# Decoder stage of a YOCO-style step: projection units spread over twenty steps, value pages asked for one loop sooner

## The reference, cut to what matters

```python
D_MODEL, SEQ, DEC_BATCH, PAST_LEN, PAGE_SIZE = 1024, 512, 8, 2048, 128
H_B, DH_B, DV_B = 8, 64, 128          # heads, size of each of the two key maps, size of a value

kv = modulate(x, sh, sc) @ w_kv        # shared keys and values of prompt and samples
q = (modulate(x, sh1, sc1) @ w_q_b).reshape(n, t, H_B, 2 * DH_B) * (DH_B ** -0.5)

def page_step(carry, xs):              # samples: 16 pages each, of 128 positions
    phys, j = xs
    kpos = j * PAGE_SIZE + jnp.arange(PAGE_SIZE)
    dist = (qpos[:, None] - kpos[None, :]).astype(jnp.float32)
    bias = -slopes[:, None, None] * dist
    return update(carry, cache_k[phys], cache_v[phys], bias), None
...
m1, l1, a1, m2, l2, a2 = update(carry, k_new, v_new, bias)
o = a1 / l1[..., None] - lam * (a2 / l2[..., None])
```

## Time and profile before

| what | value |
|---|---|
| median of 3 runs | 1935.73 us (1934.38 to 1936.28) |
| time of the profiled execution | 1931.71 us |
| its span | 1929.8 us |
| mean granted TensorE clock | 0.885 |
| PE busy | 1521.2 us (79%) |
| DVE busy | 733.9 us (38%) |
| ACT busy | 418.1 us (22%) |
| POOL busy | 349.3 us (18%) |
| DMA | 551.66 MB, mean 286 GB/s |

### The profile page before, as it was taken

How to read it: one execution, slowest core, us unless ns; L and a number is a source line. 1 busy time by engine, 2 the same in 40 slices (tenths; PEclk the granted TensorE clock), 3 DMA queues, 4 the chain that set the end, 5 groups by cost and what they waited for, 6 DMA issues and landing times. The chain is left out here.

```text
span 1929.8 us, 22099 instructions
## 1 busy us (share of the span) xinstructions
PE 1521.2 (79%) x7374; PEld 709.2 (37%) x7375; DVE 733.9 (38%) x1284; ACT 418.1 (22%) x908; POOL 349.3 (18%) x270
## 2 busy tenths in 40 slices
PE   5899986695689999646999887777596599989950
PEld 2333335142333333203466563444343233333320
DVE  1001127675300000075846577995275300000018
ACT  1001014221121222222120002334431021212222
POOL 0000000000100000033735566650000000000004
PEclk8999998597799999967999997888798699999985
DMA  8572604604599999699789999985503499999962
GB/s 314 225 275 111 263 36 152 233 23 185 224 425 422 392 382 427 275 370 344 276 306 402 408 383 412 351 316 182 186 17 129 188 417 384 418 420 400 430 242 89
DMA packets 123149, 551.66 MB, mean 286 GB/s; under 512 B 16469, under 2 KB 46022, under 8 KB 101419
## 3 DMA queue, kind: packets, MB, share of 16 engines
q1 hardware_dynamic: 94530, 492.46, 64.4%
q10 hardware_dynamic: 19584, 37.28, 5.1%
q0 software_dynamic: 8944, 20.76, 3.0%
HBM read 521.82 MB, written 40.03 MB: 291 GB/s over the span
## 5 line engine op out<-in xcount | busy, mean ns | idle before, releaser
L1576 PE MATMUL ps<-arena_w,arena_r 128*64 128x512 f32 x1600 | 361.7, 608 | 28.8 <-issue 23.9
L1576 PEld LDWEIGHTS ps<-arena_w,arena_r 128*64 128x64 f32 x1600 | 121.1, 140 | 262.6 <-issue 256.5
L1558 PE MATMUL ps<-arena_w,arena_r 128*64 128x512 f32 x800 | 181.5, 601 | 19.4 <-ACT arena_r L1606 19.4
L1653 DVE TENSOR_TENSOR arena_r<-arena_r,ps 128x512 f32<-128x512 f32 x38 | 26.1, 687 | 419.1 <-ACT arena_r L1623 419.1
L1959 POOL TENSOR_TENSOR arena_w<-arena_w,arena_r 128x1024 f32<-128x1024 f32 x48 | 115.5, 2409 | 104.0 <-DMA arena_w<-in_cache_k_dram 103.7
L1959 POOL TENSOR_TENSOR arena_r<-arena_r 128x1024 f32<-128x1024 f32 x48 | 115.9, 2418 | 54.7 <-DMA arena_r<-in_cache_k_dram 54.6
L2012 PE MATMUL ps<-arena_w,xt 128*128 128x256 f32 x512 | 123.4, 403 | 1.4 <-ACT xt L2185 1.4
L450 PE MATMUL ps<-arena_w,xt 128*128 128x512 f32 x256 | 113.8, 600 | 1.0 <-DVE arena_w L531 0.6
L1070 PE MATMUL ps<-arena_w,xt 128*128 128x512 f32 x256 | 111.4, 593 | 0.0
L2012 PEld LDWEIGHTS ps<-arena_w,xt 128*128 128x128 f32 x512 | 102.5, 203 | 17.9 <-ACT xt L2185 1.5
L1507 POOL COPY small<-idx 128x1 int32 (+1 forms) x38 | 7.0, 184 | 516.9 <-PE ps L1524 456.0
(11 more groups left out here) (384 smaller groups left out, 1969.5 us busy)
## 6 DMA issues: line engine op xcount, KB each, us to landing
arena_w<-in_w_exp_gate_dram SPq DMA_DIRECT2D x38, 2048.0 KB, 13.6
arena_w<-in_w_exp_up_dram SPq DMA_DIRECT2D x38, 2048.0 KB, 19.1
arena_w<-in_w_exp_down_dram SPq DMA_DIRECT2D x38, 2048.0 KB, 17.5
arena_m<-in_cache_v_dram SPq DMA_DIRECT2D x128, 512.0 KB, 7.0
arena_w<-in_cache_k_dram SPq DMA_DIRECT2D x64, 512.0 KB, 9.0
arena_r<-in_cache_k_dram SPq DMA_DIRECT2D x64, 512.0 KB, 8.4
arena_w<-in_w_ada_dram SPq DMA_DIRECT2D x12, 2048.0 KB, 17.6
arena_m<-in_w_ada_dram SPq DMA_DIRECT2D x12, 2048.0 KB, 9.2
```

What stands on the lines that cost most here:

```text
L1558: last = nc.tensor.matmul(psy[c][at:at + 64, :], ht[u][:, k, 64 * (1 - a):64 * (2 - a)], wd[u][:, k, c * 512:(c + 1) * 512], start=(k == 0 ...
L1576: last = nc.tensor.matmul(ps[at:at + 64, :], xgt[u][:, k, 64 * a:64 * (a + 1)], w[u][:, k, :], start=(k == 0), stop=(k == KT - 1), tile_po ...
L1653: V.tensor_tensor(hs[u], es[u], psu[:, :], ALU.mult).then_inc(h_ok, 1)
```

## The change

`projected` is another table: step g now holds unit g-1 for g up to 5 (before: one unit at step 1, two at each of steps 2 to 5), and the other 19 units are spread over steps 6 to 20, one each, but two at steps 9, 13, 17 and 20 (before: one each at steps 6 to 20). All 24 units are still done at step 20.

In SP's loop g value group g-5 is asked for rather than g-6, and the loops end one sooner. The wait for `own_parts` is split: ahead of loop 5 for ten of them, ahead of loop 6 for all twelve. The buffers, the waits of `load_key` and `load_value`, and the steps at which PE uses the values are as before.

```diff
     def projected(self, g):
 
-        n = 2 * g - 1 if g <= 5 else g + 4
-        return range(max(n - (1 if g <= 1 or g > 5 else 2), 0), min(n, 24))
+        count = lambda g: min(g, 5) + max(min(g, 20) - 5, 0) * 19 // 15
+        return range(count(g - 1), count(g)) if g >= 1 else ()
...
-            for g in range(2, NKQ + LAG):
-                if g == LAG:
-                    sp.wait_ge(sp_mm, NCH)
+            for g in range(2, NKQ + LAG - 1):
+                v = g - LAG + 1
+                if v in (0, 1):
+                    sp.wait_ge(sp_mm, NCH - 2 + 2 * v)
                 for j in range(GRP):
                     if g < NKQ:
                         load_key(GRP * g + j)
-                    if g >= LAG:
-                        load_value(GRP * (g - LAG) + j)
-                if g >= LAG and (g - LAG) % 4 == 2:
-                    b = (g - LAG) // 4
+                    if v >= 0:
+                        load_value(GRP * v + j)
+                if v >= 0 and v % 4 == 2:
+                    b = v // 4
                     if b == 0:
                         sp.wait_ge(nv_out, 32)
                     sp.dma_start(vn, m.newD[1][b:b + 1, :]).then_inc(vn_in, 16)
```

## The result

The changed kernel takes 2015.0 us (median of 3 runs, 2012.6 to 2016.83), against 1935.73 before: a ratio of 1.0413 (95% interval 1.0393 to 1.0434), 79.3 us slower. The profiled execution took 2012.6 us, its span is 2010.7, its mean granted clock 0.866 (before 0.885). The forecast was 1988, so the direction held and the loss was half again as large as its +52.8; the time lies 3 us inside the upper end of the range, 2018.

What follows compares the result with a forecast made beforehand. The prediction took full DMA engines to bound steps 9 to 20 and DVE the later steps. Its terms, 39.8 + 5 + 3 + 5 = +52.8 us on 1935.7, gave 1988 us, range 1950 to 2018.

Steps and rivals of the forecast that it cites:

- The start: Start of the stage: fewer units at steps 3 and 4 let SP resume at 961.4 instead of 973.9, gaining 12 us.
- E6: End of PE's values in step 6, the first values of the stage: forecast at 977.5.
- R: Time from end of values in step g-1 to PE's possible start of step g+1: 18.5 us, bounds 15.9 and 22.6.
- Step 9: Eight transpositions and two units, with ACT's copies behind the exponent: values end at 1041.5, before 1036.1.
- E8: End of PE's values in step 8: E6 + R + 9.4, forecast at 1005.4.
- The clock: PE units behind long waits run slower, about one more such unit per group: 3 x 1.5, +5 us (0 to 8).
- Behind step 20: Later multiplication at the end of step 21, +5 us (4 to 8), and later keys afterwards, +3 (0 to 8).
- E20: End of PE's values in step 20: 1206.8, before 1167.0, +39.8 us (bounds +29.4 and +56.2).
- Faster: Rival: DMA alone sets the pace and the hole at the start stays closed, 1917 to 1923 us; chance 0.09.
- No change: Rival: the gain at the start and the coupling cancel, R about 9, 1936 us; chance 0.02.
- mild: Rival: ACT isn't held at step 9 and groups take 53 us instead of 59, about +25, 1961 us; chance 0.13.
- Worse than the bounds: Rival: keys late at every attention step too, one us at each of 15 steps, +95, 2031 us; chance 0.04.

Runs made afterwards that it cites:

- e2: The kernel before with only the change's new SP queue (queue only), its old table of units kept: 1989.76 us, ratio 1.0293.
- e8: The changed kernel, but loop g asks for key pages 4g+1 to 4g+4 and then for its four value pages: 1956.31 us, ratio 1.0109.
- e3: The changed kernel, but each loop asks for its four key pages first, then its four value pages (keys first): 1989.31 us, ratio 1.0284.
- e4: The changed kernel with the first double step at 7 instead of 9, leaving one unit at step 9: 1990.41 us, ratio 1.0289.
- table only: The kernel before with only the change's new table of projection units, SP's queue as before: 1941.31 us, ratio 1.0038.

## Why the prediction was right, and where its size was off

**The chain.** It was named as it is: values of step g-1, keys of step g and the first of g+1 behind them in SP's queue, sums, `biggest`, PE's step g+1. e2 shows that the queue edit alone closes it, e8 that taking the keys out from behind the wait opens it, e3 that both the four keys and the fifth must come out. Most signs forecast came: value pages asked for in loop 5, ACT idle over 8 us ahead of step 9's `exponent` (12.46), groups of four steps longer than 50 us (61.1 and 69.0, forecast 59.2). PE's waits for `biggest` at steps 8, 12, 16 and 20 were forecast at some 9 us and were 11.76, 10.49, 19.42 and 11.68. The DMA share was 0.75, not 0.85. SP's waits came to 209.4 us, but the forecast "from 73 us to well over 120" started from the wrong number: both kinds of wait were 111.1 us to 1360 (117.3 to 1440), so before as well SP ran against PE more than the prediction says, and just over 120 would have been no sign.

**The start.** SP resumed at 969.41, not 961.4. The stage itself began 2.6 us later in this run. PE's step 3 is not in this path, since PE waited 5.42 us for `biggest` behind it. But `biggest`, which the prediction took over from before, ended 5.7 us later (957.67 instead of 951.96), 3.1 of them beyond the stage's own; and the unit of step 4 took 9.33 us instead of 7.0:

```profile
957.73 0.38 PE L2051 MATMUL ps<-ident,small 128*16 128x128 f32 x1 [5.42 <-DVE small L2361]
957.90 9.33 PE L2005 MATMUL ps<-xt,arena_w 128*128 128x512 f32 x16
```

E6 was 985.5 instead of 977.5: 5.4 us of the miss, after taking off the 2.6. The 3.1 us arise ahead of what the change touches. Eight small operations of DVE in step 1 (L2473), beside GpSimd's multiplications, took 12.87 us in this run and 12.88 in those of queue only and keys ahead, but 8.24 to 8.26 in before and in the six others. After and keys ahead have the latest step 6 of all kernels with the new table (89.7 and 91.0 in the table above). What decides between the two lengths is open.

**R, the term that was mis-sized.** The term that failed is "from the multiplication to the end of `common` 2.8", used for every return, and with it the 18.5 taken for R. Steps 8, 12, 16 and 20 wait for `biggest`, whose tail behind that multiplication is longer: a sum, a one-row copy (L2358), an addition and the maximum. Row by row for step 12 (the fifth key issued, its multiplication, the maximum, PE):

```profile
1074.01 0.36 SPq L1893 DMA_DIRECT2D arena_w<-in_cache_k_dram  x1
...
1080.82 1.22 DVE L2340 TENSOR_TENSOR arena_w<-arena_w,arena_r 128x1024 f32<-128x1024 f32 x1 [2.46 <-DMA arena_w<-in_cache_k_dram]
...
1084.32 0.61 DVE L2361 TENSOR_REDUCE small<-arena_r 128x16 f32<-128x272 f32 x1
...
1084.98 0.38 PE L2051 MATMUL ps<-ident,small 128*16 128x128 f32 x1 [10.49 <-DVE small L2361]
```

| before step | values end to fifth key issued | to its multiplication | to the end of `biggest` | R |
|---|---|---|---|---|
| 8 | 8.4 | 6.3 | 6.1 | 20.9 |
| 12 | 8.7 | 6.8 | 4.1 | 19.7 |
| 16 | 11.0 | 11.4 | 6.1 | 28.6 |
| 20 | 9.0 | 6.2 | 6.1 | 21.3 |
| mean | 9.3 | 7.7 | 5.6 | 22.6 |
| taken | 8.2 | 7.5 | 2.8 | 18.5 |

(In the last row 7.5 is what the 18.5 leave for the landing.) The landing, which the prediction thought its doubtful part, was right in the mean. The tail was short by 2.8; in the kernel before it stands at 4.1, 4.1, 6.1 and 6.2 us for the same steps and could have been read there. The issues were short by 1.1, most of it ahead of step 16, where two of them took 0.92 and 1.51 us. Four returns at 4.1 more make 16.4 us. Step 16's excess has a neighbour in the DMA issues of 1110 to 1160 us (KB each, us to landing):

```profile
out_k_prompt_dram<-arena_w ACTq DMA_DIRECT2D x1, 2048.0 KB, 19.1
```

```profile
1126.00:1155.00 29.00, 9.58 (x55) 6.63 (x51) 12.27 (x14) 0.58 (x1) 12.36 (x6) 0.74 1.01 390
```

The store of the prompt's keys filled the DMA engines (1.01) just while the eight pages of that loop were asked for. That it cost the 5 us or so by which this landing exceeds the others is read from the overlap, not tested.

**Step 9.** E8 + 36.1 was forecast, 35.6 measured; e4 puts its avoidable part at 21 us by the trace and 25 by the medians.

**The clock.** +5 was forecast. Apart from R, the pieces from step 6 to step 20 exceed their forecast by 4.5 us in all. That this meets the term is in part luck. Units behind a long wait took 8.90, 8.88, 9.72 and, as a double, 16.46 us instead of 7.15 and 14.05, and those of steps 10 and 14 took 8.81 and 8.86: some 12 us more in all. Against it stand pieces that were forecast too long, such as the 1.5 us of waiting ahead of steps 13 and 17, of which nothing was seen. The price per unit was 1.7 to 2.6 us rather than 1.4.

**Behind step 20.** The multiplication of step 21 began at 1252.54, 16.9 us after E20 (before 9.4): +7.5 for the +5 taken. All that follows E20, to the end of the span, cost 12.3 us where 8 were forecast.

**The sum.** Start 5.4, R 16.4, step pieces -0.5 against the +5 (4.5 measured), behind step 20 4.3, and the stage's own later start of 2.6: 28.2 us over the 52.8 is 81.0, against 80.9 between the two spans; the medians differ by 79.3. The upper bound of +80 had R at 22.6, which turned out to be the mean. So the mechanism is shown and the direction is no luck, but a measured time just inside the range is: 5.7 us of the miss lie ahead of anything that the change touches (the later stage and the longer chain of DVE), and of R only the landing was sized right.

**The rivals.** "Faster" needed R = 5.4; its early gain was real (20.5 us at step 6 by the table), and gone by step 9. "No change" and "mild" needed groups of 50 and 53 us. "Worse than the bounds" asked a microsecond at each attention step; 8.3 us were lost in the eight steps from 20 to 28, of which 7.5 stood at the multiplication of step 21 already, and 3.2 in the nine from 28 to 37.

**What stays open.** Keys ahead (e8) is 23 us over before, and 15 over table only. Its PE still waits 17.0 us for `common` and its DMA share is 0.85. The keys of step g+1 now stand behind the values of step g-1, a longer loop of the same kind, which fits; no run separates it from value traffic that crowds the keys.

## What to carry to other kernels

Asking for a page one step sooner into the same number of buffers moves its wait for a buffer one step sooner as well, and with it everything behind it in that in-order queue; check whether what the next step needs stands behind such a wait, and put it ahead if so. When pricing such a return, follow the tail of the consumer that is really waited for (here `biggest`, 6.1 us, and not `common`, 2.8). A second unit of work belongs where the engine waits anyway, and not behind an instruction that hangs on the same loop: here that was worth 21 to 25 us for one moved unit.

## What the runs showed of the hardware

**A copy that lasts as long as its neighbour.** The one-row copy L2358 on DVE takes 0.16 us or 2.13. The rows of DVE and POOL at steps 11 and 15:

```profile
1083.64 0.16 DVE L2358 COPY arena_r<-small 1x16 f32<-1x16 f32 x1
1084.26 2.35 POOL L1960 TENSOR_TENSOR arena_w<-arena_w,arena_r 128x1024 f32<-128x1024 f32 x1 [4.48 <-DMA arena_w<-in_cache_k_dram]
```

```profile
1151.42 2.34 POOL L1960 TENSOR_TENSOR arena_w<-arena_w,arena_r 128x1024 f32<-128x1024 f32 x1 [2.83 <-DMA arena_w<-in_cache_k_dram]
1151.65 2.13 DVE L2358 COPY arena_r<-small 1x16 f32<-1x16 f32 x1
```

In the second the copy ends at 1153.78, POOL's multiplication at 1153.76; in the first POOL stood still. Of the eight copies of the trace, the four of 2.13 or 2.14 us and one of 0.83 began inside a multiplication of POOL and ended within 0.05 us of it, and the three of 0.16 or 0.17 began while POOL was idle. The sums beside it (L2348, one input, 1.22 us) show no such stretch. The addition behind the copy (two inputs) was not touched in this run (0.42 us, eight times), but took 2.54 in most returns of keys first. The Trainium skill (GPSIMD Engine Reference, section on specifications) says that GpSimd's SBUF interfaces are shared with VectorE and that they contend when a DVE instruction runs in a mode with two ports or has two inputs in SBUF. For the addition and for the sums the traces agree; for the copy they fit, with at most 2 us each time, but no view shows the mode of an instruction. It is 2 us of R at three of four returns.

**The clock behind a wait.** Windows over the units of steps 12, 16 and 17 of the changed kernel:

```profile
1084.00:1095.00 11.00, 10.02 (x45) 7.73 (x49) 6.41 (x7) 0.58 (x1) 7.04 (x3) 0.78 0.75 292
1155.00:1166.00 11.00, 11.00 (x45) 8.29 (x49) 7.17 (x8) 0.59 (x1) 3.79 (x2) 0.75 0.15 61
1165.00:1182.00 17.00, 17.00 (x94) 12.99 (x90) 3.88 (x4) 1.97 (x4) 7.57 (x4) 1.00 0.68 248
```

The granted clock is 0.78 and 0.75 over the units that follow waits of 10.49 and 19.42 us, a mixture of the levels 1.2 and 2.4 GHz, and 1.00 over the next two units. The four waits ahead of steps 8, 12, 16 and 20 thus cost PE 1.7 to 2.6 us more than themselves. The length of the last wait doesn't decide it alone: behind waits of 1.25, 1.16 and 1.16 us the units of steps 10, 14 and 18 took 8.81, 8.86 and 7.17 us.
